# The low parts of the weights written over the raw weights, and rings of four

## The reference

```python
def first_block(x, c, ...):
    mod = silu(c) @ w_ada + b_ada                        # 2048 x 12288, one row
    h = rms_norm(x, g_pre_mix) * (1.0 + sc1) + sh1
    p = h @ w_in + b_in                                  # 2048 x 9216: six branches, three gates
    y = (g_sgu * (y_sgu @ w_sgu_out) + g_moba * (y_moba @ w_moba_out)
         + g_pool * (y_pool @ w_pool_out)) @ w_out
    x = x + gt1 * rms_norm(y, g_post_mix)
    z = (rms_norm(x, g_pre_ffn) * (1.0 + sc2) + sh2) @ w_up   # 2048 x 11264
    gate, val = split(causal_conv3(z))
    return x + gt2 * rms_norm((gelu(gate) * val) @ w_down, g_post_ffn)

def second_block(x, ...):
    z = rms_norm(concat(meta, x)) @ w_in_2               # 272 rows: q and kv latents, u, two gates
    mixed = sigmoid(g0) * (attention(q, kv) @ w_attn_proj) + sigmoid(g1) * glu(gelu(s5_scan(u)))
    h = h + mixed @ w_out_2
    h = h + (silu(m @ w_ffn_gate) * (m @ w_ffn_up)) @ w_ffn_down     # m = rms_norm(h)
    return rms_norm(h, norm_final)
```

## Time and profile before

| what | value |
|---|---|
| median of 3 runs | 3385.28 us (3383.56 to 3387.97) |
| the profiled execution | 3385.71 us, span 3383.9 us |
| mean granted clock of TensorE | 0.958 |
| busy share: PE, PEld, DVE, ACT, POOL | 93%, 79%, 53%, 38%, 10% |
| DMA | 671.30 MB, 198 GB/s over the span |

### The profile page before, as it was taken

One profiled execution on the slowest core, in us unless ns is written; L12 is line 12 of the kernel. 1 busy time (PEld: TensorE's weight loads), 2 busy tenths in 40 slices (PEclk: granted clock), 3 DMA queues, 4 the chain that ended last, 5 costly groups with the idle time before them and its releaser, 6 DMA issues.

```text
span 3383.9 us, 43971 instructions
## 1 busy us (share of the span) xinstructions
PE 3133.2 (93%) x18157; PEld 2664.1 (79%) x18157; DVE 1807.5 (53%) x1732; ACT 1273.0 (38%) x1151; POOL 328.3 (10%) x458
## 2 busy tenths in 40 slices
PE   8899999995999999999698999989987999999998
PEld 3577767774999999877477887777866999999776
DVE  1376666687566665544534436664544444444444
ACT  0233444333434444333322433333433444444333
POOL 1000000001000000000102916640000000000000
PEclk9999999998999999999798999999998999999999
DMA  9875666784554454555434652215543455555554
GB/s 356 295 273 226 250 244 250 275 349 180 195 213 189 197 220 168 212 200 207 160 118 156 222 200 84 71 69 199 212 159 137 172 181 188 181 185 197 199 199 149
DMA packets 110404, 671.30 MB, mean 198 GB/s; under 512 B 23488, under 2 KB 25664, under 8 KB 33216
## 3 DMA queue, kind: packets, MB, share of 16 engines
q1 hardware_dynamic: 101584, 626.96, 50.7%
q0 software_dynamic: 8704, 42.70, 3.4%
HBM read 652.22 MB, written 17.40 MB: 198 GB/s over the span
## 4 chain that ended last, share of the span: by engine, by line
PE 73%; DVE 15%; ACT 7%; issue 3%; DMA 1%; POOL 0%; DVEq 0%; ACTq 0%; SPq 0%; POOLq 0%
PE acc L1780 22%; PE acc L1781 21%; PE acc L1782 21%; DVE w_lo L1115 6%; ACT w_hi L752 5%; PE ms L1850 3%; PE tp L1825 2%; DVE bias_rows L1408 2%; DVE mod_sum L1190 1%; PE acc L2255 0%; DVE y L1156 0%; DMA w_raw<-w_stream 0%; DMA w_raw<-ada_stream 0%; ACT L752 0%; DVE ssm_z L1599 0%
## 5 line engine op out<-in xcount | busy, mean ns | idle before, releaser
L1115 DVE TENSOR_TENSOR w_lo<-w_raw,w_hi 128x2048 fp32r<-128x2048 f32 x484 | 1116.4, 2307 | 1225.5 <-ACT w_hi L752 1214.3
L752 ACT ACTIVATE w_hi<-w_raw 128x2048 fp32r<-128x2048 f32 x484 | 926.2, 1914 | 1628.0 <-PE acc L1782 1456.5
L1780 PE MATMUL acc<-h2T_hi,w_lo 128*128 128x256 f32 x2816 | 797.6, 283 | 36.2 <-DVE w_lo L1115 31.7
L1782 PE MATMUL acc<-h2T_hi,w_hi 128*128 128x256 f32 x2816 | 793.7, 282 | 0.0
L1781 PE MATMUL acc<-h2T_lo,w_hi 128*128 128x256 f32 x2816 | 793.4, 282 | 0.0
L1780 PEld LDWEIGHTS acc<-h2T_hi,w_lo 128*128 128x128 f32 x2816 | 536.4, 190 | 41.9 <-DVE w_lo L1115 38.1
L1781 PEld LDWEIGHTS acc<-h2T_lo,w_hi 128*128 128x128 f32 x2816 | 536.7, 191 | 0.0
L1782 PEld LDWEIGHTS acc<-h2T_hi,w_hi 128*128 128x128 f32 x2816 | 536.6, 191 | 0.0
L1780 PE MATMUL acc<-w_hi,hid_lo 128*128 128x512 f32 x704 | 281.1, 399 | 7.3 <-DVE w_lo L1115 7.2
L1781 PE MATMUL acc<-w_lo,hid_hi 128*128 128x512 f32 x704 | 278.8, 396 | 0.0
L1782 PE MATMUL acc<-w_hi,hid_hi 128*128 128x512 f32 x704 | 278.8, 396 | 0.0
(11 more groups left out here) (512 smaller groups left out, 4042.4 us busy)
## 6 DMA issues: line engine op xcount, KB each, us to landing
w_raw<-w_stream SPq DMA_DIRECT2D x484, 1024.0 KB, 4.8
ada<-ada_stream SPq DMA_DIRECT2D x64, 1024.0 KB, 6.9
w_raw<-ada_stream SPq DMA_DIRECT2D x32, 1024.0 KB, 4.9
g_dram<-gates_out SPq DMA_DIRECT2D x12, 512.0 KB, 6.8
gates_in<-g_dram POOLq DMA_DIRECT2D x12, 512.0 KB, 4.6
bias_rows<-b_in POOLq DMA_DIRECT2D x18, 256.0 KB, 4.4
x_res<-x POOLq DMA_DIRECT2D x2, 2048.0 KB, 13.9
g_dram<-gate_stage SPq DMA_DIRECT2D x8, 512.0 KB, 2.9
```

The lines of the kernel that those rows point to most:

```text
L752: sc.activation(whi[:, s % 2], raw[:, s % 4], ACT.Copy).then_inc(hi_made, 1)
L1115: v.tensor_tensor(wlo[:, s % 2], raw[:, s % 4], whi[:, s % 2].bitcast(F32), ALU.subtract).then_inc(lo_made, 1)
L1780: mm(o, sl, mh, start=start, stop=False, skip_group_check=share)
L1782: return mm(o, sh, mh, start=False, stop=stop, skip_group_check=share)
```

## The change

The raw weights and the low parts share one set of four buffers: DVE writes the low part over the raw values that it reads. The 16 KB per partition that the two low buffers had go to the high parts, which get four buffers as well. So a slot of the ring is raw, then low, and is free when TensorE has ended the group; `load` therefore waits for `pe_used` in place of `lo_made`. A high part of group n has its buffer free whenever the raw weights of group n have landed (their load waited for TensorE's end of n-4), so ACT's wait for `pe_used` is taken out.

```diff
         raw = at("w_raw", [P, 4, GK, C], 0)
-        whi = at("w_hi", [P, 2, GK, C], 32, F32R)
-        wlo = at("w_lo", [P, 2, GK, C], 48, F32R)
+        whi = at("w_hi", [P, 4, GK, C], 32, F32R)
+        wlo = at("w_lo", [P, 4, GK, C], 0, F32R)
...
             for s in range(G_IN1):
-                sp.wait_ge(lo_made, s + 1)
+                sp.wait_ge(pe_used, s + 1)
                 load(s % 4, a["w_stream"][s + 4])
...
                 act.wait_ge(raw_in[s % 4], (up + (N_FRONT + s) // 4 + 1) * 16)
-                if not m.early(2):
-                    act.wait_ge(pe_used, m.n - 1)
-                sc.activation(whi[:, s % 2], raw[:, s % 4], ACT.Copy).then_inc(hi_made, 1)
+                sc.activation(whi[:, s % 4], raw[:, s % 4], ACT.Copy).then_inc(hi_made, 1)
...
                 dve.wait_ge(hi_made, m.n + 1)
-                v.tensor_tensor(wlo[:, s % 2], raw[:, s % 4], whi[:, s % 2].bitcast(F32), ALU.subtract).then_inc(lo_made, 1)
+                v.tensor_tensor(wlo[:, s % 4], raw[:, s % 4], whi[:, s % 4].bitcast(F32), ALU.subtract).then_inc(lo_made, 1)
...
             def begin_group():
                 pe.wait_ge(lo_made, m.n + 1)
-                return m.slot % 2
+                return m.slot % 4
```

More of the change, by code:

```diff
@@ L350, in _ @@
             for s in range(G_MERGE):
-                sp.wait_ge(lo_made, G_IN1 + s + 1)
+                sp.wait_ge(pe_used, G_IN1 + s + 1)
                 load(s % 4, a["w_stream"][G_IN1 + s + 4])
@@ L360, in _ @@
                 g_ = G_IN1 + G_MERGE + s
-                sp.wait_ge(lo_made, g_ + 1)
+                sp.wait_ge(pe_used, g_ + 1)
                 load(s % 4, a["w_stream"][g_ + 4])
@@ L368, in stream @@
                     for j in range(4):
-                        sp.wait_ge(lo_made, i * 4 + (g0 + j + 1))
+                        sp.wait_ge(pe_used, i * 4 + (g0 + j + 1))
                         load(j, row(a["w_stream"], i * 4 + (g0 + j + 4)))
             def one(g_):
-                sp.wait_ge(lo_made, g_ + 1)
+                sp.wait_ge(pe_used, g_ + 1)
                 load(g_ % 4, a["w_stream"][g_ + 4])
@@ L384, in _ @@
                     for q in range(4):
-                        sp.wait_ge(lo_made, i * 8 + (g_up + 4 + 4 * j + q + 1))
+                        sp.wait_ge(pe_used, i * 8 + (g_up + 4 + 4 * j + q + 1))
                         load(q, row(a["w_stream"], i * 8 + (g_up + 8 + 4 * j + q)))
@@ L2146, in q_rope @@
             def q_rope(j):
-                s = m.slot % 2
+                s = m.slot % 4
                 if j:
```

## The result

| what | before | after |
|---|---|---|
| median | 3385.98 us (3383.56 to 3387.97, 4 executions) | 3257.73 us (3256.88 to 3261.18, 4 executions) |
| ratio | | 0.9623, 95% interval 0.9607 to 0.964 |
| the profiled execution, its span | 3385.71 us, 3383.9 us | 3258.35 us, 3256.6 us |
| mean granted clock of TensorE | 0.958 | 0.970 |

The account below looks back on a forecast made before the run. The prediction took TensorE, busy 93% of the span, as the bound. Its terms 44.7 + 30.3 + 5 + 22.6 + 12.7 + 2 = 117.3 us, off 3385.3, gave 3268 us, range 3258 to 3310.

Parts of the forecast that it names:

- spare: Weight ring: time between a group being ready and TensorE wanting it, 8.1 us after the change against 1.5 before.
- First up projection: First up projection: all 31.1 us of waits for low parts go, with 13.6 us of clock dips; -44.7 us.
- First attention and `mod_cols`: First attention: eight waits for scaled scores and their clock dips go, -30.3 us; the `mod_cols` wait shrinks, -5.
- Ends of stages: Six stage ends: the copy no longer waits behind the next splits, 4.15 us at five and 1.8 at one; -22.6.
- Other waits for a low part: Elsewhere: waits of 8.6 and 4.4 us stay, latent projection gives -6.8 with its dip, small ones -5.9; -12.7 us.
- First output projection: First output projection: a load of 13.67 us exceeds what the ring allows; between 0 and -8.7, taken as -2 us.
- In-place write: VectorE's split writing over its input: taken to need 2.29 us as between two buffers, so costed at nothing.
- the clock: TensorE's granted clock: dips behind the waits go with them, 28.9 us of the sum.
- (1): First input stage: another wait takes over, for `ada` data or weights; 35.3 us stay, 3303 us; chance 0.17.
- (2): TensorE's clock is not regained: waits shrink but dips stay; 28.9 us stay, 3297 us; chance 0.10.
- (3): Weight loads come too late beside the second stream: slower, up to 3514 us; chance 0.04.
- (4): The change does nothing, since program order keeps the splits' lead at two groups; chance 0.03.

Follow-up runs that it names:

- wait_n1: Kernel after, with ScalarE's wait for TensorE's end of group n-2 put back; four buffers and in-place write stay: 3391.05 us, ratio 1.0016 to the kernel before.
- wait_n2: Kernel after, with a ScalarE wait for TensorE's end of group n-3, one group looser than before the change: 3261.34 us, ratio 0.9637 to the kernel before.
- late_loads: Kernel after, with every weight load outside the heads waiting for TensorE's end of one group later: 3390.25 us, ratio 1.0023 to the kernel before.
- in1_wait: Kernel after, with ScalarE's old wait put back for groups 4 to 71 alone, first input projection with first attention: 3295.05 us, 37.3 us over after.
- ends_wait: Kernel after, with ScalarE's old wait put back for twelve groups, the first two behind each of six stage ends: 3285.81 us, 28 us over after.
- up1_wait: Kernel after, with ScalarE's old wait put back for groups 102 to 187 alone, in the first up projection: 3311.45 us, 53.7 us over after.
- sp_order: Kernel after, with two weight loads moved on SP's queue ahead of the block storing and fetching the scan's output: 3266.95 us; run again, 3256.13 us.

## Why the prediction was right, and where it was off

- **The lead, not the buffers.** Right: the ring's arithmetic put the pair ahead of the chunk's end, and wait_n1 (late, no gain) and wait_n2 (early, all of it) show that this is what counts. The prediction gave a "spare" of 8.1 us against 1.5; the pair against the chunk's end would have been the sharper number, since it says that late_loads loses and the spare (2.4 us there) doesn't. How much late_loads loses neither of them says.
- **First up projection, -44.7.** Measured 550.7 - 503.9 = 46.8 in the traces. The 31.1 us of waits all went, and TensorE's busy time there fell by 519.5 - 503.9 = 15.6 us, where the 8 dips made 13.6.
- **First attention and `mod_cols`, -35.3.** Measured 37.3 by in1_wait, 38.4 between the first matmul and the first output projection in the traces (559.5 to 521.1 us). The eight waits went, the one for `mod_cols` fell from 4.2 to 0.3 us.
- **Ends of stages, -22.6.** The four largest fell by 4.2, 3.3, 4.1 and 4.2. ends_wait gives 28 by the medians and 23.8 by the profiled executions, 21.0 of it idle TensorE and 2.8 slower matmuls: the term was right, without a clock part. (A small slip: the rows give 806.61 - 802.37 = 4.24, not 4.15, from TensorE's end to the copy; over five ends 0.4 us.)
- **Other waits for a low part, -12.7.** The 8.6 us stayed as 8.2 and the 4.4 as 4.6, as forecast. Missed was the wait of 4.0 at the attention projection. The prediction had costed the second attention and SP's queue at nothing, "in steady state"; this place isn't steady, a block of stores stands there, and where the kernel after waits 4.0 us behind it, the kernel before had 2.5 us, 45 us later.
- **First output projection, -2.** The stretch from its first matmul to the up projection shrank by 142.6 - 136.9 = 5.7 us; 4.15 of it is the end of the stage, so 1.6 are left.
- **In-place write, 0.** `w_lo` takes 2310 ns on average over all 484; a split took 2.29 alone. Right.
- **The step that was mis-sized is the clock:** 28.9 us in the sum, 41.6 in TensorE's busy time. Dips were counted only behind the waits in the first up projection, the first attention and the latent projection. Stage by stage the busy time fell by 533.7 - 520.7 = 13.0 us from the first input projection to the first output projection (11.9 in the sum), by 15.6 in the first up projection (13.6), by 545.7 - 538.2 = 7.5 from the second input stage to the attention projection (3.4), and by 5.5 in all the other stages, for which the sum had none. What it costs was not the same everywhere: for each us of wait that was put back, slower matmuls added 15.3 / 31.2 = 0.49 us in up1_wait's stage and 13.2 / 22.9 = 0.58 in in1_wait, but 2.8 / 21.0 = 0.13 in ends_wait. In those ends TensorE stands idle for up to 26 us even in the kernel after, so the clock may be low behind them either way; that reason was not tested. Of the 12.7 us some may be chance, since the second attention alone was busy 211.5 to 224.4 us in different executions.
- **Rivals.** (1) did happen as a mechanism and not as a price: VectorE waits 38.8 us for `ada` data, where 8.2 was all its idle time there before, over the 20 us that the prediction had set as a sign that it was wrong. In the first attention TensorE's only wait for VectorE is 0.3 us. The sign was badly chosen: an engine with 1.4 us in hand at each chunk's end, as in the timeline above, can wait for data; the same wait read on TensorE would have been a sign. late_loads shows the other side: 100.4 us of it in the first input stage, which got 12 us slower than before. (2) fell: the clock came back, and more than was counted. (3) fell as a whole: the landing is 4.8 us in the median as before; it stands in the one stall. (4) fell.

## What to carry to other kernels

Read a ring of buffers by what stands behind its pair in the queues: work out when the last split ahead of a copy is ready against the end of the chunk that the copy empties, and look at the sign. If it is late, every emptying and every stage end pays for it, and in a dense stream of matmuls a clock dip besides; once it is early, more lead gives nothing (wait_n2 against after). Buffers alone buy nothing if a wait still holds the engine back: here the four buffers were worth nothing until the wait fell, and with two the wait couldn't fall, since ScalarE would write over a high part that TensorE still reads. And when the ring is long enough, look for order in a wait that stays: two changes of order gave 17 us more.

## What the runs showed that was not expected

A load one group later, 5.7 us, cost the whole 128 us, though by the ring's arithmetic a group is still ready 2.4 us before TensorE wants it; in part this came through the other stream, whose data VectorE then waited for. Sixteen stores issued one after the other held SP's queue for 11.06 us, 0.69 us each, and the weight loads behind them with it. And a short wait of TensorE can cost more than its length: the 16 waits of 31.2 us in up1_wait brought 15.3 us of slower matmuls with them, 0.49 us for each us of wait. With no such wait in between, the granted clock over 390 us of the first attention was 1.00, and 0.96 with the eight waits. In the heads, where TensorE is idle for a tenth of the time, the same matmuls ran at 0.95, 0.92 or 0.89 in different executions and took 232 to 245 us. Between the two profiled executions of sp_order (3266.59 and 3261.35 us) the heads differ by 6.7 us, more than the times do; its other executions have no profile.
